# Routing weights as a table in list order, and a column copy per expert in place of a gather

## What is computed

```
e_sel  = logits of the 8 experts of the token's best group      # top-1 group of 4
top_v, top_i = lax.top_k(e_sel, 2)                              # top-2 experts in it
ew     = softmax(top_v) * g_w                                   # a weight for each of the 2 choices
# for each of 32 experts, over the tokens that chose it:
hb     = silu(x @ w_gate[e]) * (x @ w_up[e])                    # 1024 -> 512
y_row  = (hb @ w_down[e]) * weight                              # 512 -> 1024
y[token] = sum of its 2 rows;   x = x + y;   final rmsnorm
```

## Time and profile before

| | |
|---|---|
| Times of three runs | 1165.65, 1168.63, 1169.9 us (median 1168.63) |
| Profiled execution | 1170.12 us, its span in the trace 1168.3 us |
| TensorE busy | 1142.2 us, 98% of the span |
| DVE, ACT, POOL busy | 856.8 (73%), 688.7 (59%), 257.5 (22%) us |
| DMA | 324.09 MB, 277 GB/s mean; 380 to 400 GB/s through the experts |
| Mean granted TensorE clock | 0.995 |

### The profile page before, as it was taken

How to read it: one execution, slowest core, us unless ns; L and a number is a source line. 1 busy time by engine, 2 the same in 40 slices (tenths; PEclk the granted TensorE clock), 3 DMA queues, 4 the chain that set the end, 5 groups by cost and what they waited for, 6 DMA issues and landing times.

```text
span 1168.3 us, 18090 instructions
## 1 busy us (share of the span) xinstructions
PE 1142.2 (98%) x5934; PEld 962.3 (82%) x5934; DVE 856.8 (73%) x1340; ACT 688.7 (59%) x1134; POOL 257.5 (22%) x348
## 2 busy tenths in 40 slices
PE   7999999999999999999999999999999999999997
PEld 7988888888889888887788888888888888888873
DVE  6649510134447766667899999999999999999966
ACT  6341241223437744334687887887877877878834
POOL 2200210001200012223242322323323323323320
PEclk9999989999999999999999999999999999999999
DMA  8212240436969644453999999999999999999998
GB/s 234 78 36 83 90 136 1 128 141 207 316 236 370 227 145 145 149 195 139 408 379 388 394 384 406 382 398 393 380 396 387 384 396 388 393 398 388 386 266 348
DMA packets 110146, 324.09 MB, mean 277 GB/s; under 512 B 22454, under 2 KB 59232, under 8 KB 85520
## 3 DMA queue, kind: packets, MB, share of 16 engines
q1 hardware_dynamic: 92384, 279.17, 64.4%
q0 software_dynamic: 17712, 44.27, 10.5%
HBM read 285.37 MB, written 51.12 MB: 288 GB/s over the span
## 4 chain that ended last, share of the span: by engine, by line
PE 89%; DMA 6%; DVE 2%; ACT 1%; issue 1%; SPq 0%; POOL 0%; POOLq 0%; DVEq 0%; ACTq 0%
PE psum L935 26%; PE psum L937 26%; PE psum L936 25%; PE psum L1219 2%; DMA units<-mlstm_units 2%; PE psum L1253 1%; PE psum L1125 1%; PE psum L1297 1%; PE psum L1060 1%; DMA w_row<-entry_weights,first_row 1%; PE psum L1061 1%; PE psum L1106 1%; PE psum L981 1%; DMA e_st<-expert_rows 1%; PE psum L949 1%
## 5 line engine op out<-in xcount | busy, mean ns | idle before, releaser
L2035 DVE TENSOR_TENSOR e_lo<-e_st,e_hi 128x1024 fp32r<-128x1024 f32 x384 | 444.5, 1219 | 10.8 <-ACT e_hi L1531 10.7
L1531 ACT ACTIVATE e_hi<-e_st 128x1024 fp32r<-128x1024 f32 x384 | 375.8, 1052 | 9.7 <-DMA e_st<-in_expert_w_gate_dram 4.6
L937 PE MATMUL psum<-e_hi,ex_lo 128*128 128x512 f32 x512 | 199.4, 390 | 0.0
L935 PE MATMUL psum<-e_hi,ex_hi 128*128 128x512 f32 x512 | 199.4, 389 | 0.1
L936 PE MATMUL psum<-e_lo,ex_hi 128*128 128x512 f32 x512 | 199.2, 389 | 0.0
L935 PE MATMUL psum<-xT_hi,w_hi 128*128 128x512 f32 (+1 forms) x432 | 151.5, 351 | 2.2 <-DVE w_lo L1671 1.4
L936 PE MATMUL psum<-xT_lo,w_hi 128*128 128x512 f32 (+1 forms) x432 | 149.6, 346 | 0.0
L937 PE MATMUL psum<-xT_hi,w_lo 128*128 128x512 f32 (+1 forms) x432 | 149.5, 346 | 0.0
L935 PEld LDWEIGHTS psum<-e_hi,ex_hi 128*128 128x128 f32 x512 | 96.1, 188 | 20.5 <-DVE ex_lo L2106 0.5
L937 PEld LDWEIGHTS psum<-e_hi,ex_lo 128*128 128x128 f32 x512 | 96.1, 188 | 20.0
L936 PEld LDWEIGHTS psum<-e_lo,ex_hi 128*128 128x128 f32 x512 | 96.1, 188 | 19.9
(11 more groups left out here) (292 smaller groups left out, 1858.9 us busy)
## 6 DMA issues: line engine op xcount, KB each, us to landing
e_st<-in_expert_w_gate_dram SPq DMA_DIRECT2D x64, 1024.0 KB, 8.0
e_st<-in_expert_w_up_dram SPq DMA_DIRECT2D x64, 1024.0 KB, 9.4
e_st<-in_expert_w_down_dram SPq DMA_DIRECT2D x64, 1024.0 KB, 10.9
mlstm_units<-stage SPq DMA_DIRECT2D x18, 640.0 KB, 3.7
w_st<-in_w_in_dram SPq DMA_DIRECT2D x20, 512.0 KB, 4.4
xn_scratch<-xn POOLq DMA_DIRECT2D x20, 512.0 KB, 3.9
stage<-gate_rows SPq DMA_DIRECT2D x18, 512.0 KB, 5.8
e_st<-expert_rows SPq DMA_DIRECT2D x15, 512.0 KB, 8.8
```

The costliest lines, as they stand in the source:

```text
L935: pe.matmul(out, a_hi, b_hi, start=start, stop=False)
L937: return pe.matmul(out, a_lo, b_hi, start=False, stop=stop)
L1531: act.activation(e_hi[:, r, :, :], e_st[:, slot, :, :], ACT.Copy).then_inc(ehi_done, 1)
L2035: dve.tensor_tensor(e_lo[:, r, :, :], e_st[:, slot, :, :], e_hi[:, r, :, :].bitcast(F32), ALU.subtract).then_inc(elo_done, 1)
```

## The change

A second table in DRAM, `list_w_dram` (`row_list_weights`), has the layout of `list_dram` and holds weights. It is filled with zeros (line 803 of the changed kernel), and for each choice k and block t GpSimd scatters the 128 weights `choice_w[:, k, order[t]]` to the places `slot_i[:, t, k]`: 20 indirect DMAs, in two groups of ten. One DMA of GpSimd then loads the whole table into `weights_to`, in which column i holds the 128 weights of step i. From step 4 on, `weights_copied` copies that column into `w_row[:, b]`; the gathers of steps 0 to 3 stay. The wait of `rows_in` on the earlier weight gather goes. `choice_w` comes from two more DVE operations. The last column of `rows_to` is set by GpSimd instead of the DVE.

```diff
+    list_w_dram = nc.dram_tensor("row_list_weights", (CAP * E, 1), F32).ap()
+    choice_w = const("choice_w", [P, 2, NT])
+    weights_to = mbuf("weights_to", [P, NT * E + 1])
...
             pool.dma_start(list_dram.rearrange("(q n) a -> q (n a)", q=80), sentinel[:, :]).then_inc(table_set, 16)
+            pool.dma_start(list_w_dram.rearrange("(q r n) a -> q r (n a)", q=64, n=P),
+                           zero_row[:, :].unsqueeze(1).broadcast_to([64, E * CAP // 64 // P, P])).then_inc(table_set, 16)
...
-            pool.wait_ge(table_set, 16)
+            pool.wait_ge(table_set, 32)
...
                 else:
-                    pool.wait_ge(factor_in[b], slot_loads(i - 2, b))
-                    pool.sem_inc(pool_past, 1)
                     pool.tensor_copy(row_of[:, b:b + 1], rows_to[:, bass.ds(i, 1)]).then_inc(row_picked, 1)
...
+            def listed_weights(k):
+                for t in range(NT):
+                    pool.indirect_dma_start(
+                        out=list_w_dram, out_offset=bass.IndirectOffsetOnAxis(ap=slot_i[:, t, k:k + 1], axis=0),
+                        in_=choice_w[:, k, order[t]:order[t] + 1], in_offset=None).then_inc(table_set, 16)
+
+            def weights_copied(i, b):
+                pool.tensor_copy(w_row[:, b:b + 1], weights_to[:, bass.ds(i, 1)]).then_inc(row_weighted, 1)
...
-            pool.wait_ge(table_set, 32)
+            pool.wait_ge(table_set, 48)
             pool.wait_ge(first_rows, 16)
             rows_in(1, 1)
             weights_in(0, 0)
             weights_in(1, 1)
-            pool.wait_ge(no_row, 1)
+            pool.memset(rows_to[:, NT * E:NT * E + 1], 2 * T).then_inc(pool_step, 1)
+            pool.memset(weights_to[:, NT * E:NT * E + 1], 0.0).then_inc(pool_step, 1)
+            pool.wait_ge(pool_step, 24)
             pool.wait_ge(later_rows, 16)
             rows_in(2, 0)
             rows_in(3, 1)
+            listed_weights(0)
             rows_out(0, 0)
             weights_in(2, 0)
             weights_in(3, 1)
             rows_in(4, 0)
+            listed_weights(1)
+            pool.wait_ge(table_set, 16 * (3 + 2 * NT))
+            pool.memset(weights_to[:, NT * E:NT * E + 1], 0.0).then_inc(pool_step, 1)
+            pool.wait_ge(pool_step, 23)
+            pool.dma_start(weights_to[:, 0:NT * E].rearrange("p (r e) -> p r e", e=E),
+                           list_w_dram.rearrange("(r p e) a -> p r (e a)", p=P, e=E)).then_inc(table_set, 16)
             rows_out(1, 1)
-            weights_in(4, 0)
+            pool.wait_ge(table_set, 16 * (4 + 2 * NT))
+            weights_copied(4, 0)
             n_half = load_half_steps(pool)
             with pool.Fori(2, n_half) as j:
                 rows_in(2 * j + 1, 1)
                 rows_out(2 * j - 2, 0)
-                weights_in(2 * j + 1, 1)
+                weights_copied(2 * j + 1, 1)
                 rows_in(2 * j + 2, 0)
                 rows_out(2 * j - 1, 1)
-                weights_in(2 * j + 2, 0)
+                weights_copied(2 * j + 2, 0)
...
             def hidden(i, b):
                 dve.wait_ge(sg_done, i + 1)
-                dve.wait_ge(factor_in[b], slot_loads(i, b))
+                if isinstance(i, int):
+                    dve.wait_ge(factor_in[b], slot_loads(i, b))
+                else:
+                    dve.wait_ge(row_weighted, i - 3)
...
             link(dve.reciprocal(wts[:, 0, :], wts[:, 2, :]))
+            dve.tensor_copy(choice_w[:, 0, :], wts[:, 0, :])
+            dve.tensor_tensor(choice_w[:, 1, :], wts[:, 0, :], rd21[:, :], ALU.mult)
...
-            dve.memset(rows_to[:, NT * E:NT * E + 1], 2 * T).then_inc(no_row, 1)
```

More of the change, by code:

```diff
@@ L314, in build @@
         gx_load = [sem(f"gx_load{i}") for i in range(2)]
-        ehi_done, elo_done, piece_used, no_row, gx_zero, ext_ready, exhi_done, exlo_done = (
-            sem(n) for n in ("ehi_done", "elo_done", "piece_used", "no_row", "gx_zero",
+        ehi_done, elo_done, piece_used, row_weighted, gx_zero, ext_ready, exhi_done, exlo_done = (
+            sem(n) for n in ("ehi_done", "elo_done", "piece_used", "row_weighted", "gx_zero",
                              "ext_ready", "exhi_done", "exlo_done"))
@@ L863, in weights_in @@
             def weights_in(i, b):
[L865 to L868, removed]
+                rows = rows_to[:, i:i + 1] if i else first_row[:, :]
                 pool.indirect_dma_start(
@@ L1809, in gate_rows_stabilised @@
                 link(dve.tensor_copy(mlast[:, :], m_end))
-                dve.wait_ge(table_set, 16)
+                dve.wait_ge(table_set, 32)
                 by_direction(lambda r, o, i: dve.tensor_scalar(negm_rows[r, o], g_m[r, i], -1.0, None, ALU.mult))
```

## The result

| | kernel before | changed kernel |
|---|---|---|
| median of 9 runs each, same chip | 1166.48 us (1164.5 to 1169.98) | 1175.43 us (1173.4 to 1180.91) |
| ratio | | 1.0076, 95% interval 1.0062 to 1.0090 |
| profiled execution | 1170.12 us | 1177.88 us |
| its span | 1168.3 us | 1176.1 us |

The change costs 8.9 us. The forecast was 19 us: the sign was right, the size less than half right. The 1175.43 us lies in the range 1174 to 1197, near its lower end.

The account below looks back on a forecast made before the run. It took TensorE, without idle time in the loop, as the bound. 0 in the loop, +17.4 us at expert 5's transposes and +1.6 clock made 19.0 us, put on the median of 1168.63: 1188 us, range 1174 to 1197.

Parts of the forecast that it names:

- No gain in the loop: Expert loop: removing 28 word gathers of 1.98 us each on GpSimd gains 0, since TensorE has no idle time.
- the removed wait: In rows_in: dropping the wait on the earlier weight gather gains 0, because nothing was waiting there.
- The cheap additions: Zero fill, two DVE operations and two GpSimd memsets before the experts, one-column copies in the loop: each costs 0.
- Which work blocks which: GpSimd's queue: scatters, load and two waits delay the gather of expert 5; TensorE stalls some 15 us before its transposes.
- The spacing of the scatters: Twenty new scatters on GpSimd before the loop: 2.25 us apart, with 1.32 and 2.28 kept as bounds.
- a stall of 2.1 us at expert 2: TensorE at expert 2: a first stall of 2.1 us, because its weight gather queues behind the first ten scatters.
- the rival of short spacing: Scatters at 1.72 or 1.32 us apart: the first ten hide wholly, time 1175 to 1181 us; chance 0.17.
- The landings: GpSimd's two waits before the gather of expert 5: last scatter lands in 8.1 us, table load in 9.3 us.
- 17.4 us of lateness: Transposes of expert 5: their gathered rows land at 651.5 us, wanted at 634.1, so 17.4 us late.
- the two ends that I worked out for short spacing: Lateness at expert 5 with shorter scatters: 10.2 us at 1.72 us spacing, 6.6 us at 1.32 us.
- The clock: TensorE right behind the stall at expert 5: a lower clock for a while, costing 1.6 us.
- The end: Behind the loop: the five adds start at most 2.3 us earlier without the last gather; taken as 0.

Follow-up runs that it names:

- e3: Kernel before without the 28 weight gathers of the loop and with no table in their place, so later weights are wrong: 1167.69 us, 0.9993.
- e8: Kernel before with one extra 1.5 MB store in SyncE's queue ahead of the loads of step 2, without scatters: 1170.46 us, 1.0024.
- e7: Changed kernel with the gather of expert 5 ahead of the second ten scatters, GpSimd's loop order kept from step 6 on: 1171.25 us, 1.0035.
- e1: Kernel before plus the twenty scatters, zero fill and two DVE operations; table never read, waited for only behind the loop: 1175.51 us, 1.0066.
- e1_again: The same kernel as e1, run once more in another session for a second trace: ratio 1.0041 to the kernel before.
- e2: Changed kernel with the gather of expert 5 moved ahead of the second ten scatters, GpSimd's loop turned by one gather to match: 1171.58 us, 1.0031.
- e4: Changed kernel with 30 scatters in the second group in place of 10, the added ones into spare tables nobody reads: 1199.44 us, 1.0265.
- e5: Changed kernel, scatters regrouped 12 + 8, weight of expert 4 still gathered, gather of expert 5 before the table wait, copies from expert 5 on: 1176.39 us, 1.0071.
- e9: Changed kernel with one extra 1.5 MB store in SyncE's queue ahead of the loads of step 2: 1178.47 us, 1.0099 to the kernel before.

## Why the prediction was half right

- **No gain in the loop, none from the removed wait: right.** e3, 0.9993.
- **The cheap additions: right.** Expert 1 starts at 567.49, against 567.61. The 1.07 us at expert 2 is a clock of 0.93 and 0.80 (560 to 575 us) behind a wait of 2.50 us that the kernel before has too (2.27 us) without this loss; such a loss comes and goes between traces (e8, e7 and e3 have one, e1 has not, e1_again has), and it costs nothing here because GpSimd's chain ends later anyway.
- **Which work blocks which: right.** Gather of expert 5 behind the table's load, one stall there, released by the DMA of gx, the clock low behind it, all later steps at 17.75. e2 takes the stall away by one moved call, and e4 delays the gather one for one (27.3 us for 26.8 us of scatters).
- **The spacing of the scatters: the step that failed.** I took 2.25 us from the earlier trace rows and held 1.32 us from the earlier trace rows as the bound. Measured 1.44 and 1.70 on average. The first ten so cost nothing where I had rows_out(0) 2.4 us late and a stall of 2.1 us at expert 2 (its hh started at 602.68, and the stall was 0.2 us). The last scatter started at 616.06, not 622.6: -6.5 us. Three rows in a stretch of 6 us were too few to set a price over 45 us. L820 was the same kind of transfer, and I gave the case that rested on it, the rival of short spacing with 1175 to 1181 us, 0.17. That case is what came, at its lower edge.
- **The landings: both too long.** Last scatter 7.1 us (taken 8.1), load of the table 5.9 us (taken 9.3; 7.8 in e7 and 7.3 in e2): -4.4 us. The copies ahead of the gather took 2.9 in place of 2.1 us, +0.8. Sum: 642.7 - 6.5 - 4.4 + 0.8 = 632.6, as measured, and the gather landed in 9.0 us (taken 8.8). 17.4 us of lateness became 7.5, which is between the two ends that I worked out for short spacing, 6.6 and 10.2.
- **The clock: too small.** 1.6 us taken from the earlier trace rows, 2.6 and 1.6 measured in the two traces.
- **The end: taken as 0, measured -1.8.** 1.7 of it is the low clock of the earlier trace rows, which this trace lacks, and that is luck: the same wait of about 2 us is followed here by a clock of 1.00. The adds start earlier relative to the last transposes (5.5 us ahead in place of 3.5), as foretold, and gain nothing.
- **What the prediction did not have at all: the DMA debt of the scatters**, 2 to 5 us. I wrote that the scatters move almost no bytes, which is true, and took them as free for the DMA. It does not show in the changed kernel, whose stall pays it by the account above. A forecast of e2 or e5 made with the same steps would have said 1.000 and missed by 4 to 8 us.

So the 8.9 us are the late gather (7.5, shown by e2 and e4) and the clock behind it (some 2), with the debt hidden under the stall. That the scatters cost time by themselves is shown by e1, twice; that they do it through the DMA rests on the late loads, the bytes moved and e8, which shows that a debt is kept but not one of this size. No arrangement of the table that I tried is faster than the kernel before; with the loop's gain at nothing, there was none to be had.

## What to carry over

Work that is queued ahead of a prefetch delays it by the whole chain, waits and landings included: put the next gather ahead of such work, as e2 does by one line, before costing anything else. In these runs, with the DMA at a share of 1.00 beside a full TensorE, 10 KB of scatters cost as much transfer as 0.8 to 1.9 MB: look at the DMA time of a transfer and not only at its bytes. And the price showed up far from the cause, at the first place where nobody is ahead any more. And where two prices for an instruction lie in the trace, a handful of rows from one moment of a periodic stretch is a bound, not the likely value.

## What the runs showed of the hardware

- Scatters of 128 words mostly take about 1.3 or 2.3 us from start to start on GpSimd. What decides is open. It is not the place in the step of 17.8 us: in the changed kernel those from 576.42 to 582.86 are short, and those from 611.51 to 616.06, two steps later, are long. It is not that DVE runs `e_lo` alone either: it did so without a gap from 571.77 to 581.71, beside two long scatters and four short ones.
- Twenty scatters of 10 KB in all kept the DMA engines busy (share 0.9 to 1.1) while the throughput fell from 395 to 298 GB/s in the window from 580 to 590 us of the changed kernel.
- The same idle stretch of TensorE has different consequences: 2.27 us gave 0.68 and 0.50, 2.07 us at the same place of the changed kernel 1.00; 2.69 us in e9 1.00, 5.99 and 7.98 us gave 0.53 and 0.57, and 24.77 us in e4 0.55. Of the short ones it can't be said beforehand.
- A POOL copy of one column can take 5.6 to 10.0 us once in a run (e1, e2, e5). Not explained.
